# The first two modulation sections of a two-block transformer kernel: from sums on VectorE to products on TensorE, tile by tile

## The reference, cut to what matters

```python
mod = jnp.einsum('bd,ldm->lbm', jax.nn.silu(c), w_mod) + b_mod[:, None, :]
for i in range(DEPTH):
    sh_m, sc_m, g_m, sh_f, sc_f, g_f = [t[:, None, :] for t in jnp.split(mod[i], 6, axis=-1)]
    h = x * (1.0 + sc_m) + sh_m
    ...
        y = even_mixer(h, cos, sin, w_in_even[i // 2], w_out_even[i // 2])
```

## Time and profile before

| | us |
|---|---|
| median of 3 runs | 1303.54 (1301.99 to 1307.19) |
| the profiled execution's own time | 1302.91 |
| span of its trace | 1300.9 |
| TensorE busy | 1207.7 (93% of the span) |
| VectorE busy | 895.1 (69%) |
| ScalarE busy | 603.7 (46%) |
| mean granted TensorE clock | 0.979 of full speed |

### The profile page before, as it was taken

How to read it: one execution, slowest core, us unless ns; L and a number is a source line. 1 busy time by engine, 2 the same in 40 slices (tenths; PEclk the granted TensorE clock), 3 DMA queues, 4 the chain that set the end, 5 groups by cost and what they waited for, 6 DMA issues and landing times.

```text
span 1300.9 us, 24296 instructions
## 1 busy us (share of the span) xinstructions
PE 1207.7 (93%) x9450; PEld 1175.2 (90%) x9450; DVE 895.1 (69%) x1453; ACT 603.7 (46%) x952; POOL 27.2 (2%) x49
## 2 busy tenths in 40 slices
PE   1599998999998999899999979999999999999997
PEld 1598788999998899889999969999999998999997
DVE  7589767898687786567564457866954675777633
ACT  1347625434434357454444346543433645555532
POOL 0100000000000000000000000000000000000000
PEclk9999989999999999999999989998989999999999
DMA  8754663996793433437455514532323452554530
GB/s 317 305 185 171 219 226 140 337 355 238 266 348 112 146 107 132 184 130 258 164 192 191 172 58 148 178 107 106 113 101 106 144 197 102 197 188 164 181 143 33
DMA packets 35074, 232.87 MB, mean 179 GB/s; under 512 B 4656, under 2 KB 7088, under 8 KB 7088
## 3 DMA queue, kind: packets, MB, share of 16 engines
q1 hardware_dynamic: 29232, 189.78, 40.6%
q0 software_dynamic: 5760, 41.95, 9.0%
HBM read 230.67 MB, written 1.05 MB: 178 GB/s over the span
## 4 chain that ended last, share of the span: by engine, by line
PE 83%; DVE 8%; ACT 4%; issue 3%; DMA 2%; SPq 0%; DVEq 0%; ACTq 0%
PE acc L1703 21%; PE acc L1705 21%; PE acc L1704 21%; PE aux L1703 2%; PE aux L1705 2%; PE aux L1704 2%; PE aux L2147 2%; PE aux L1796 2%; DVE qkv L1059 2%; PE aux L1776 2%; DMA cst<-consts 1%; ACT whi L475 1%; PE aux L1789 1%; DVE wlo L881 1%; PE aux L2021 0%
## 5 line engine op out<-in xcount | busy, mean ns | idle before, releaser
L1703 PE MATMUL acc<-hhi,whi 128*128 128x256 f32 (+1 forms) x1984 | 577.4, 291 | 26.5 <-DMA cst<-consts 11.4
L881 DVE TENSOR_TENSOR wlo<-raw,whi 128x1024 fp32r<-128x1024 f32 x338 | 412.7, 1222 | 244.1 <-ACT whi L475 243.3
L1704 PE MATMUL acc<-hlo,whi 128*128 128x256 f32 (+1 forms) x1984 | 570.0, 287 | 0.0
L1705 PE MATMUL acc<-hhi,wlo 128*128 128x256 f32 (+1 forms) x1984 | 568.7, 287 | 0.0
L475 ACT ACTIVATE whi<-raw 128x1024 fp32r<-128x1024 f32 x338 | 356.3, 1055 | 215.5 <-PE acc L1705 189.2
L1703 PEld LDWEIGHTS acc<-hhi,whi 128*128 128x128 f32 x1984 | 378.8, 191 | 31.6 <-issue 17.2
L1705 PEld LDWEIGHTS acc<-hhi,wlo 128*128 128x128 f32 x1984 | 380.0, 192 | 0.0
L1704 PEld LDWEIGHTS acc<-hlo,whi 128*128 128x128 f32 x1984 | 379.6, 191 | 0.5
L1703 PE MATMUL aux<-ahi,whi 128*128 (+2 forms) x264 | 74.9, 284 | 0.0
L1704 PE MATMUL aux<-alo,whi 128*128 (+2 forms) x264 | 74.8, 283 | 0.0
L1705 PE MATMUL aux<-ahi,wlo 128*128 (+2 forms) x264 | 74.8, 283 | 0.0
(11 more groups left out here) (332 smaller groups left out, 1471.1 us busy)
## 6 DMA issues: line engine op xcount, KB each, us to landing
raw<-weights SPq DMA_DIRECT2D x177, 1024.0 KB, 4.9
lev<-side_weights POOLq DMA_DIRECT2D x40, 1024.0 KB, 7.5
cst<-consts SPq DMA_DIRECT2D x1, 1608.0 KB, 14.6
x<-xT SPq DMA_DIRECT2D x1, 1024.0 KB, 7.6
out<-x SPq DMA_DIRECT2D x4, 256.0 KB, 2.2
vec<-vecs SPq DMA_DIRECT2D x1, 163.0 KB, 2.4
pos<-positions SPq DMA_DIRECT2D x1, 128.0 KB, 3.4
cst<-consts SPq DMA_DIRECT2D x1, 64.5 KB, 3.9
```

The costliest lines, as they stand in the source:

```text
L881: v.tensor_tensor(wlo[:, m % SPLIT, :], raw[:, (m + MOD_UNITS) % RAW, :], whi[:, m % SPLIT, :].bitcast(F32), ALU.subtract).then_inc(lo_rea ...
L1703: mm(o, whi[:, u % SPLIT, w], hi, start=start, stop=False, skip_group_check=True)
L1704: mm(o, whi[:, u % SPLIT, w], lo, start=False, stop=False, skip_group_check=True)
L1705: return mm(o, wlo[:, u % SPLIT, w], hi, start=False, stop=stop_, skip_group_check=True)
```

## The change

The sections 0 and 1 are laid out by output tile. A unit of "mod" now holds all 1024 rows of K for one output tile of 128 columns, and a chunk holds output tile n of section 0 and of section 1. `first_sections(n)` multiplies both on TensorE without any sum on VectorE: 16 calls with a block of `raw` as the stationary operand and one column of silu(`c`) as the moving one, accumulated over K. VectorE's `first_tile(n)` adds the result to `mods`, which holds the bias already, and makes tile n of `h`. TensorE multiplies that tile with the first three units of "even" at once (`first_products`), one tile of `h` behind the sections. The first four units of "even" (`FIRST` = 4) are loaded ahead of "mod" and are split at the start. The rest of the constants comes in three transfers in place of one, and `cst_loaded` is waited for before unit 3 of "even" in place of unit 0. GpSimd's memsets fall away, and its loads of the other sections wait for `first_mm` 7. The transposes of tile 19 move from before unit 2 to before unit 3. Sections 2 to 11 change in their numbering alone.

```diff
 CST = {}
 _at = 0
 for _name, _n in [
-    ("inv", 1), ("ones", P), ("ident", P), ("mean", P), ("mean_v", P), ("tri", P), ("neg8", P), ("rot", P), ("dup", P),
-    ("rotdup", P), ("past", 384), ("past_neg", 384), ("causal", 256), ("level", 7 * P),
-    ("fresh", T2),
+    ("inv", 1), ("ones", P), ("ident", P), ("rot", P), ("dup", P), ("rotdup", P), ("mean", P), ("mean_v", P),
+    ("tri", P), ("neg8", P), ("past", 384), ("past_neg", 384), ("causal", 256), ("level", 7 * P), ("fresh", T2),
 ]:
     CST[_name] = _at
     _at += _n
 NCST = _at
-FIRST_CST = 1 + P
+CST_PARTS = (0, CST["ident"], CST["mean"], CST["level"], NCST)
+FIRST = 4
...
+            c = 1 if i is None and m < FIRST else (m + MOD_UNITS) // RAW + 1
...
-            sp.dma_start(cst[:, 0:FIRST_CST], consts[:, 0:FIRST_CST]).then_inc(small_loaded, 16)
-            for s in range(slots):
+            def load_constants(part, signal):
+                a, b = CST_PARTS[part:part + 2]
+                sp.dma_start(cst[:, a:b], consts[:, a:b]).then_inc(signal, 16)
+
+            load_constants(0, small_loaded)
+            for s in range(3):
                 load(s, s)
-            for name, n, kind in SEGMENTS:
+            sp.dma_start(x[:, :, META:T2], xT.rearrange("p (k t) -> p k t", k=KT)).then_inc(x_loaded, 16)
+            sp.dma_start(x[:, :, 0:META], metaT.rearrange("p (k t) -> p k t", k=KT)).then_inc(x_loaded, 16)
+            load(3, 3)
+
+            for c in range(FIRST // 2):
+                sp.wait_ge(lo_ready, 2 * c + 2)
+                load(c, c + slots)
+            for c in range(FIRST // 2, CST_AT):
+                sp.wait_ge(first_mm, c - FIRST // 2 + 1)
+                load(c % slots, c + slots)
+            load_constants(1, cst_loaded)
+            for c in range(CST_AT, (FIRST + MOD_UNITS) // 2):
+                sp.wait_ge(first_mm, c - FIRST // 2 + 1)
+                load(c % slots, c + slots)
+            load_constants(2, masks_loaded)
+            for name, n, kind in SEGMENTS[1:]:
...
-                    if name == "mod" and j == slots - 1:
-
-                        sp.dma_start(x[:, :, META:T2], xT.rearrange("p (k t) -> p k t", k=KT)).then_inc(x_loaded, 16)
-                        sp.dma_start(x[:, :, 0:META], metaT.rearrange("p (k t) -> p k t", k=KT)).then_inc(x_loaded, 16)
-                if name == "mod":
-                    sp.dma_start(cst[:, FIRST_CST:], consts[:, FIRST_CST:]).then_inc(cst_loaded, 16)
+                if name == "even":
+                    load_constants(3, levels_loaded)
 
...
+            for m in range(FIRST):
+                split(None, m)
...
-            prime("even")
...
-            dve.wait_ge(pool_step, 2)
-            dve.wait_ge(csilu_ready, 1)
-            for u in range(MOD_UNITS):
-                if u % 2 == 0:
-                    dve.wait_ge(load_done[(u % RAW) // 2], 16 * (u // RAW + 1))
-                if u >= 1:
-                    dve.wait_ge(first_used, u)
-                total = mod_sums[u // KT]
-                v.scalar_tensor_tensor(total, raw[:, u % RAW, :], small[:, u % KT:u % KT + 1], total,
-                                       ALU.mult, ALU.add).then_inc(first_used, 1)
-            split(None, 0)
-            add_mods(1, 2, [(0, 8, 0), (8, 16, 1)])
+            st(v.tensor_copy(mods[:, 0:8], V("b_mod", 0, 8)))
+            st(v.tensor_scalar(mods[:, 8:16], V("b_mod", 8, 8), 1.0, None, ALU.add))
+            dve.wait_ge(trig_ready, 2)
             dve.wait_ge(x_loaded, 32)
-            h_tiles(0, T1, lambda n: modulate(0, n))
-            split(None, 1)
-            split(None, 2)
+            st.wait()
+
+            def first_tile(n):
+
+                dve.wait_ge(first_mm, n + 1)
+                pair = mods[:, n:n + 9:8]
+                v.tensor_tensor(pair, aux[n % 4][:, 0:2], pair, ALU.add).then_inc(first_mods, 1)
+                dve.wait_ge(first_mods, n + 1)
+                modulate(0, n)
+            h_tiles(0, T1, first_tile, lag=0)
...
-            pe.wait_ge(small_loaded, 32)
-            mod_section(0)
-            mod_section(1)
-            pe.wait_ge(cst_loaded, 16)
+            def first_sections(n):
+
+                c = FIRST // 2 + n
+                pe.wait_ge(load_done[c % 4], 16 * (c // 4 + 1))
+                if n >= 4:
+                    pe.wait_ge(first_mods, n - 3)
+                for s_ in range(2):
+                    u = (2 * c + s_) % RAW
+                    for k in range(KT):
+                        ins = mm(aux[n % 4][:, s_:s_ + 1], raw[:, u, P * k:P * k + P], small[:, k:k + 1], start=k == 0, stop=k == KT - 1)
+                ins.then_inc(first_mm, 1)
...
+            def first_products(k):
+
+                pe.wait_ge(h_ready, k + 1)
+                for u in range(LEAD):
+                    ins = three(ring[u][:, 0:T1], u, k, hhi[:, k, 0:T1], hlo[:, k, 0:T1], k == 0, k == KT - 1)
+                    if k == KT - 1:
+                        ins.then_inc(units_done, 1)
+
+            pe.wait_ge(csilu_ready, 1)
+            for n in range(KT):
+                first_sections(n)
+                if n == 0:
+                    pe.wait_ge(lo_ready, LEAD)
+                else:
+                    first_products(n - 1)
+            first_products(KT - 1)
+            for u in range(LEAD, SEG["even"]):
+                if u == LEAD:
+                    pe.wait_ge(cst_loaded, 16)
+                if u == STICK_AT:
+                    pe.wait_ge(masks_loaded, 16)
...
-                    if u == 0:
-                        pe.wait_ge(h_ready, k + 1)
...
-            nc.gpsimd.memset(mod_sums[0], 0.0).then_inc(pool_step, 1)
-            nc.gpsimd.memset(mod_sums[1], 0.0).then_inc(pool_step, 1)
...
-            pool.wait_ge(first_used, 14)
+            pool.wait_ge(first_mm, 7)
...
-        "mod": np.concatenate([section(0), section(1)]), "even": host_wide(even)[EVEN_TILES],
+        "mod": interleave(*(host_wide(a["w_mod"][0][:, D * n:D * n + D]) for n in range(2))),
+        "even": host_wide(even)[EVEN_TILES],
...
-    stream = np.concatenate([parts[name] for name, _, _ in SEGMENTS])
+    stream = np.concatenate([parts["even"][:FIRST], parts["mod"], parts["even"][FIRST:]] + [parts[name] for name, _, _ in SEGMENTS[2:]])
```

More of the change, by code:

```diff
@@ L35 @@
 RAW = 8
+CST_AT = 7
 SPLIT = 4
@@ L432, in _ @@
+            load_constants(1, cst_loaded)
[4 more added lines that the diff above has]
+            for name, n, kind in SEGMENTS[1:]:
                 first, split0, _ = START[name]
+                done = FIRST // 2 if name == "even" else 0
                 chunks = min(n // 2, CHUNKS - slots - first // 2)
                 def follow(i, j):
[L436 to L441, removed]
+                    sp.wait_ge(lo_ready, lin(i, split0 + 2 * j + 2))
@@ L442, in follow @@
                     load((first // 2 + j) % slots, lin(i, first // 2 + j + slots, slots))
-                rounds = chunks // slots if name != "mod" else 0
+                rounds = (chunks - done) // slots
                 if rounds:
                     with sp.Fori(0, rounds) as i:
-                        for j in range(slots):
+                        for j in range(done, done + slots):
                             follow(i, j)
-                for j in range(slots * rounds, chunks):
+                for j in range(done + slots * rounds, chunks):
@@ L475, in split @@
                 A(whi[:, m % SPLIT, :], raw[:, (m + MOD_UNITS) % RAW, :], ACT.Copy).then_inc(hi_ready, 1)
-            def prime(seg):
-                for m in range(LEAD):
-                    split(None, START[seg][1] + m)
             def segment(seg, fn, head=0, steps=None, per=0, first=None, tail=0):
@@ L487, in unit @@
                         first(j)
-                    if i is not None or m0 + j + LEAD < SPLIT_UNITS:
+                    if i is not None or FIRST <= m0 + j + LEAD < SPLIT_UNITS:
                         split(i, m0 + j + LEAD)
@@ L912, in side_sum @@
                     dve.wait_ge(side_used, n)
-                total, part = mod_sums[2 + e], mod_ring[n // 2 % 2][:, D * (n % 2):D * (n % 2) + D]
+                total, part = mod_sums[e], mod_ring[n // 2 % 2][:, D * (n % 2):D * (n % 2) + D]
                 if k:
@@ L1194, in even_then @@
                 if u == 6:
+                    dve.wait_ge(masks_loaded, 16)
                     index_scores()
@@ L1768, in mod_section @@
             def mod_section(s_):
[L1770 to L1773 removed]
+                pe.wait_ge(side_used, KT * (s_ - 1))
                 for k in range(KT):
                     q = KT * s_ + k
[L1776 removed]
+                    ins = mm(aux[3][:, q:q + 1], mod_sums[s_ - 2][:, P * k:P * k + P], C("ones", 1), start=True, stop=True)
                 ins.then_inc(mods_done, 1)
@@ L1953, in even_pieces @@
                     mod_section(3)
-            for u in range(SEG["even"]):
+            def first_products(k):
[17 more added lines that the diff above has]
+                    pe.wait_ge(masks_loaded, 16)
```

42 lines of the change are left out of this document (18 added, 24 removed).

## The result

The change made the kernel slower: 1326.79 us (median of 4 runs, 1325.63 to 1328.24) against 1305.03 us for the kernel before (median of 4 runs). The ratio is 1.0169, 95% interval 1.0143 to 1.0195. The forecast was 1324.3 us, 21.4 us above its base; the medians lie 21.8 us apart. The interval of the ratio is 18.7 to 25.4 us in time, so an agreement within 0.4 us is closer than these runs can tell, and in part luck. The profiled execution of the changed kernel took 1328.24 us and its span is 1326.4 us.

The account below looks back on a forecast made before the run. TensorE was taken as the bound. 13.0 + 8 x 6.88 + 8 x 1.92 = 83.4 us, plus 0.2 and 0.3, put unit 3 at 83.9, 21.4 us later: 1302.91 becomes 1324.3 us, range 1313 to 1330.

Parts of the forecast that it names:

- What bounds the start before: Start of the kernel before: TensorE idles 33.1 us for VectorE's sums, then 11.4 us for the constants; first product at 51.62.
- The slow price of a call: First sections on TensorE: instructions start 0.215 us apart at the slow clock, so one tile's 32 take 6.88 us.
- The slow clock: Changed start: one-column calls do not keep the clock up, so all eight tiles take the slow price.
- Its two pieces of evidence: Earlier trace: clock 0.57 on average after one-column calls from 164.60 us, and the section at 186 us at 0.50.
- When TensorE starts: First "mod" chunk lands at 13.0 us; the second at about 18, ahead of need at 19.9, and loads stay ahead.
- The sum to unit 3: Start to unit 3 of "even": 83.4 us plus 0.2 and about 0.3, so 83.9 in place of 62.46.
- The late return of the clock: Around unit 3: clock may return only 4.4 us after the last one-column call, against 3.84 us of products; about 0.3 us.
- Costs at nothing: During the start: making `h`, the splits, constants and GpSimd's multiplication and loads are covered, taken as zero.
- Behind unit 3: After unit 3 of "even": same work in the same order, so the old distances stay.
- B: Eight tiles of the start: clock rises in some, 4.1 us back per tile; with four, 1308 us; chance 9%.
- C: Start: clock fast from tile 2 on, unit 3 at 54.0, 8.4 us earlier than before, 1294.5 us; chance 5%.
- D: Behind unit 2: new wait from bunched splits or the clock's late return, 3 to 6 us more, 1327 to 1331; chance 6%.

Follow-up runs that it names:

- e4: Kernel before with only the constants changed: two transfers, 512 columns ahead of the twelfth chunk, the rest behind it; 1295.17 us, ratio 0.9943.
- e2: Changed kernel with the products of units 0 to 2 moved behind the sections of all eight tiles; 1322.22 us, ratio 1.0153.
- e8: Changed kernel with 12 unread products of 256 float32 columns on TensorE ahead of the sections; 1322.73 us, one run.
- e1: Changed kernel with a moving operand of 128 columns in place of one in each first-section call; 1298.1 us, ratio 0.995.
- e3: Changed kernel with half of the section calls, K tiles 0 to 3 only, so sums lack half their terms; 1305.11 us, one run.
- e10: Changed kernel, unchanged, profiled once more; 1323.13 us, one run.
- e11: Kernel before, unchanged, profiled once more; 1302.81 us, one run.
- e5: Kernel before with a moving operand of 128 columns of ones in place of one in the mod_section calls; 1297.4 us, ratio 0.9963.

## Why the prediction was right, point by point

- **What bounds the start before** was right and is shown in its parts: with the constants out of the way the product starts 10.0 us earlier (e4).
- **The slow price of a call** was right: 0.215 us forecast, 54.74 us for 256 in one piece (e2), that is 0.214.
- **The slow clock** was right. Of its two pieces of evidence one was weaker than it says: the section at 186 us, recorded at 0.50, stands behind a wait of 2.08 us that the prediction does not name. The fall at 168 us, with no wait ahead, carries the reading. The changed kernel's own record could not show it: 22 to 31 us reads 1.00 there, just as 24 to 26 did in the earlier trace rows. The prediction had asked for a record near 0.50 "from its first record on", and no first record came before the rise. e8 makes one happen, and then 0.50 stands there at the same distances between calls. e1 shows the other direction.
- **When TensorE starts**: 13.0 forecast, 12.91 measured. The one chunk that could be late was not, with 6.8 us of calls ahead of it; e3 and e8 show that it would be with 3.6. It came closer than forecast: about 18 against a need at 19.9, where in e3 and e8 it was there at 19.1 and 19.0 and the changed kernel needed it at 19.7.
- **The sum to unit 3**: 83.9 forecast, 83.31 measured. A tile's cycle was 8.74 us, forecast 8.80.
- **The late return of the clock** was the term with the wrong size: it came at 85.16, 6.1 us after TensorE turned from the last one-column call to products at 79.04, and not 4.4. Eight products of unit 3 were slow, some 0.8 us in place of 0.3. Those 0.3 us, worked out as 4.4 us against 3.84 us of products, lie behind the start of unit 3, and the sum puts them before it. The term also has no fixed size. In e10, the same program, the last group of products starts at 79.40 and the clock is back 4.0 us later, before unit 3:

```profile
83.17 0.40 PE L1712 MATMUL acc<-hhi,wlo 128*128 128x256 f32 x1
...
83.74 0.28 PE L1711 MATMUL acc<-hlo,whi 128*128 128x256 f32 x1
```

In e10 unit 4 starts at 88.00, 21.2 us behind the first execution of the kernel before, in the other 21.7; the forecast of 21.4 lies between the two.
- **Costs at nothing**: the splits, `h` and the constants cost nothing. TensorE has no wait for any of them up to 100 us; GpSimd's multiplication stretched one step of `h` to 2.60 us and stayed under the calls. The prediction misread the queue in one point: it has the 512 columns of constants issued at about 71 us. They wait for the fifth tile's calls and not a later tile's, and were issued at 53.34, which only gave them more room:

```profile
53.34 0.43 SPq L429 DMA_DIRECT2D cst<-consts  x1
```

- **Behind unit 3** nothing was to change, and the prediction named a change there as a sign of being wrong. At unit 4 the distance is 21.7 us, at 399 us 21.2. The 4.1 us in the profiled execution after that are clock, and e10 and e11 show such shifts between executions of one program. Against the first execution of the kernel before, the changed kernel lost 2.9 us or more between 399 and 546 us in both of its executions, and the kernel before 4.6 us in one of two; whether the shifted start makes such falls likelier stays open.
- **Rivals**: B, C and D did not occur: all tiles took the slow price (groups 8.74 or 8.75 us apart to the last), and TensorE waited for nothing between 13 and 100 us. C was close to what a small edit makes: with 128 columns, unit 3 starts at 55.24, where C had said 54.0. The rule of the Trainium skill ("TensorE: Matmul & The Clock Gate", "Why this matters for your kernels") that a TensorE kept busy runs at the fast clock does not hold for these calls: busy 20.00 us of 20, granted 0.50 (e8).

## What to carry to other kernels

Before work is moved from VectorE to TensorE, price its calls at both clocks and look in the trace for the clock behind calls of the same form; here the slow price made 55 us of what would have been 29. A float32 call with a one-column moving operand took as long as one with 128 columns, and only the second brought the clock up, so columns that nobody reads can make it faster. When a change has several parts, run each alone: the transfer of the constants was worth 8 us by itself and was buried under the rest.

## What the runs showed of the hardware that I had not expected

- 32 instructions of a 128x128 float32 block with 128 moving columns took 3.48 us, and with one column 3.59 us, both at the fast clock.
- The granted clock reads 1.00 up to the first recorded fall, even while TensorE runs slow. In the changed kernel that covers 70 us in which calls lay 0.214 us apart. In e5, with a fall recorded earlier, the same products read 0.50 that read 1.00 in the kernel before.
- Dense 128x1 sections with no wait ahead were followed by a fall of the clock 26 times of 27, the same sections with 128 columns none of 12. A section of 16 instructions by itself, at 638.90 in the kernel before, left it at 1.00.
- After a run of one-column calls the clock came back after 6.1 us of products in one execution of the changed kernel and after 4.0 us in the other.
- Two executions of the kernel before, with spans 0.1 us apart, stood 4.6 us apart at 546 us: the granted clock falls at other places from one execution to the next.
